# A two-block layer: even blocks of the modulation product, first products without the norm, and 32 in place of 28 quarter units ahead of the neighbourhood attention

## What is computed

```python
u = rmsnorm(h, norm_mix_pre)
proj = u @ w_in
q_na, k_na, v_na, q_gl, k_gl, v_gl, g_gl, z_gl = parts
o_na = rmsnorm(neighbourhood_attention(q_na, k_na, v_na, rpb), na_gain)
o_gl = gla_bidirectional(q_gl, k_gl, v_gl, g_gl, z_gl, ...)
h = h + rmsnorm(concatenate([o_na, o_gl]) @ w_o, norm_mix_post)
...
mod = silu(c) @ w_ada + b_ada
```

## Time and profile before

| | |
|---|---|
| median of three runs | 1654.26 us (1652.23 to 1655.45) |
| the profiled execution | 1651.1 us |
| its span, first to last instruction | 1649.3 us |
| mean granted clock of TensorE | 0.959 |
| TensorE busy | 1541.9 us, 93% |
| VectorE, ScalarE, GpSimd busy | 846.0, 630.7, 563.6 us |
| HBM read | 151.89 MB, 93 GB/s over the span |

### The profile page before, as it was taken

The page is one execution under the profiler, slowest core; times in us unless marked ns, Lnnn a source line. Parts: engine busy times, 40 slices in busy tenths (PEclk is TensorE's granted clock), DMA queues, the critical chain, the costliest instruction groups (busy, mean ns, idle before and its releaser), DMA issues.

```text
span 1649.3 us, 20836 instructions
## 1 busy us (share of the span) xinstructions
PE 1541.9 (93%) x8734; PEld 1303.8 (79%) x8734; DVE 846.0 (51%) x1081; ACT 630.7 (38%) x1008; POOL 563.6 (34%) x231
## 2 busy tenths in 40 slices
PE   4979899987999999998999998999988999999996
PEld 4978788886999999876768766777876888888885
DVE  3243232425788888744569757863454343342122
ACT  4452534644333333322342345345444333233231
POOL 2321121131444444533324422222442444444441
PEclk9999899797999999999799998999998999999998
DMA  4211111011222232766222211111221333332332
GB/s 178 90 52 40 39 63 67 22 65 39 91 90 91 95 96 92 258 243 241 86 77 90 94 60 51 65 52 51 90 77 63 129 115 128 111 99 97 103 102 77
DMA packets 43628, 155.32 MB, mean 94 GB/s; under 512 B 4848, under 2 KB 5488, under 8 KB 43536
## 3 DMA queue, kind: packets, MB, share of 16 engines
q1 hardware_dynamic: 42960, 151.51, 26.8%
q10 hardware_dynamic: 576, 2.49, 0.4%
HBM read 151.89 MB, written 2.10 MB: 93 GB/s over the span
## 4 chain that ended last, share of the span: by engine, by line
PE 84%; ACT 6%; DVE 5%; DMA 2%; issue 1%; POOL 0%; SPq 0%; DVEq 0%; ACTq 0%
PE G L410 72%; DMA raw<-wstream 2%; PE B L387 2%; PE B L857 1%; PE B L877 1%; DVE ada_acc L1712 1%; PE B L769 1%; PE G L643 1%; PE B L602 1%; ACT whi L954 1%; PE G L550 1%; PE G L867 1%; PE G L645 1%; PE B L515 1%; PE B L619 0%
## 5 line engine op out<-in xcount | busy, mean ns | idle before, releaser
L367 POOL TENSOR_TENSOR wlo<-raw,whi 128x1024 fp32r<-128x1024 f32 x227 | 563.4, 2485 | 1058.0 <-ACT whi L954 1058.0
L410 PE MATMUL G<-uhi,whi 128*128 128x258 f32 (+4 forms) x1920 | 539.0, 333 | 36.9 <-DVE ulo L1437 12.3
L410 PE MATMUL G<-ulo,whi 128*128 128x258 f32 (+4 forms) x1920 | 527.0, 327 | 0.0
L410 PE MATMUL G<-uhi,wlo 128*128 128x258 f32 (+4 forms) x1920 | 525.9, 326 | 0.0
L410 PEld LDWEIGHTS G<-uhi,whi 128*128 128x128 f32 x1920 | 325.4, 192 | 104.1 <-issue 67.4
L410 PEld LDWEIGHTS G<-uhi,wlo 128*128 128x128 f32 x1920 | 325.6, 192 | 30.1
L410 PEld LDWEIGHTS G<-ulo,whi 128*128 128x128 f32 x1920 | 325.5, 192 | 28.1
L954 ACT ACTIVATE whi<-raw 128x1024 fp32r<-128x1024 f32 x227 | 239.4, 1055 | 222.7 <-DMA raw<-wstream 222.5
L410 PE MATMUL G<-yhi,whi 128*128 128x512 f32 x352 | 142.0, 404 | 12.5 <-POOL wlo L367 12.5
L410 PE MATMUL G<-ylo,whi 128*128 128x512 f32 x352 | 141.4, 402 | 0.0
L410 PE MATMUL G<-yhi,wlo 128*128 128x512 f32 x352 | 140.9, 400 | 0.0
(11 more groups left out here) (266 smaller groups left out, 1588.8 us busy)
## 6 DMA issues: line engine op xcount, KB each, us to landing
raw<-wstream SPq DMA_DIRECT2D x227, 512.0 KB, 3.3
ada_in<-ada SPq DMA_DIRECT2D x40, 512.0 KB, 5.9
ada_late<-ada SPq DMA_DIRECT2D x8, 512.0 KB, 3.6
h<-hT SPq DMA_DIRECT2D x8, 264.0 KB, 4.5
out<-res SPq DMA_DIRECT2D x8, 256.0 KB, 2.1
biasn<-bias SPq DMA_DIRECT2D x2, 960.0 KB, 10.8
...
```

Of the source, the lines that this page charges most:

```text
L367: pool.tensor_tensor(wlo[:, i, :], raw[:, i, :], whi[:, i, :].bitcast(F32), ALU.subtract)\
L410: ins = pe.matmul(dst[:, x, 0:xw], w[:, slot, b * P:(b + 1) * P], u[:, k, off + x0:off + x0 + xw], start=(first and i == 0 and j == 0), st ...
```

## The change

The first products use `h * gain` without the root; the copy out of PSUM multiplies each token by its root instead. Lists and buffers: g comes first among the mixed units, 32 pieces run ahead of the neighbourhood attention, squares have three buffers, `tx` has four and lies where q comes later. SP's order at the start and the steps of the modulation blocks change, and DVE splits the first two units in place of POOL.

```diff
-MIXED = [("q", 0), ("k", 0), ("v", 0), ("g", 0), ("g", 1), ("g", 2), ("g", 3),
+MIXED = [("g", 0), ("g", 1), ("g", 2), ("g", 3), ("q", 0), ("k", 0), ("v", 0),
          ("q", 1), ("k", 1), ("v", 1), ("q", 2), ("k", 2), ("v", 2), ("q", 3), ("k", 3), ("v", 3)]
-GLA_PIECES = 28
-NA_SHARE = [3, 2, 3, 2, 3, 3, 2, 3, 2, 3, 3, 3, 2, 2, 0, 0, 0, 0]
+GLA_PIECES = 32
+NA_SHARE = [2, 2, 2, 2, 2, 3, 3, 2, 2, 3, 3, 3, 2, 1, 0, 0, 0, 0]
...
+def ada_by(j):
+
+    return min(ADA_EARLY, ADA_RING + 5 * j // 3)
...
+        sg = sb("sg", [P, 4, T], arena(o))
+        zT = sb("zT", [32, T], arena(o))
+        sq1 = sb("sq1", [P, 3, T], arena(o + 2112)); o += 8448
...
+        tx = sb("tx", [P, 4, T], arena(0)); o += 4224
...
+        rstd1 = sb("rstd1", [P, T], arena(o)); o += 2112
...
+        ADDED = ("mix_pre", "mix_post", "ffn_post", "ffn2", "final")
...
-            for k in range(KD):
-                sp.dma_start(h[:, k, :], hT[:, k, :]).then_inc(s[f"h_in{k % 2}"], 16)
-            sp.dma_start(vec[:, :], vecs).then_inc(s["vec_in"], 16)
-            sp.dma_start(ones[:, :], consts[:, P:2 * P]).then_inc(s["ones_in"], 16)
+            sp.dma_start(vec[:, 0:KD], vecs[:, 0:KD]).then_inc(s["pre_in"], 16)
+
+            def load_h(k):
+                sp.dma_start(h[:, k, :], hT[:, k, :]).then_inc(s[f"h_in{k}"], 16)
...
-            for n in range(RING):
-                load_unit(n)
+            load_unit(0)
+            load_h(0)
+            load_unit(1)
+            load_h(1)
+            load_h(2)
+            for k in range(3, KD):
+                sp.wait_ge(s[f"h_in{k - 3}"], 16)
+                load_h(k)
+            sp.dma_start(vec[:, KD:NVEC], vecs[:, KD:NVEC]).then_inc(s["vec_in"], 16)
+            sp.dma_start(ones[:, :], consts[:, P:2 * P]).then_inc(s["ones_in"], 16)
+            sp.wait_ge(s["h_in5"], 16)
+            load_unit(2)
+            sp.dma_start(upt[:, :], up).then_inc(s["up_in"], 16)
+            sp.dma_start(scan_keep[:, :, :], scanm).then_inc(s["gla_in"], 16)
+            load_unit(3)
+            sp.wait_ge(s["unit_in2"], 16)
             sp.dma_start(ident[:, :], consts[:, 0:P]).then_inc(s["ident_in"], 16)
-            sp.dma_start(scan_keep[:, :, :], scanm).then_inc(s["gla_in"], 16)
...
-                    for x in range(ADA_RING + 2 * j - 2, min(ADA_EARLY, ADA_RING + 2 * j)):
+                    for x in range(ada_by(j - 1), ada_by(j)):
...
-            for n in range(NUNIT):
+            pool.wait_ge(s["unit_split"], 2)
+            for n in range(2, NUNIT):
```

```diff
+            two_tiles(U0["z"], T0["z"], lambda k: split_ready("mix_pre", k))
+
+            def half_tile(dst, n, half):
+
+                unit_ready(n)
+                ins = product(dst, n % RING, [(k, k) for k in range(4 * half, 4 * half + 4)], uhi, ulo, 0, T,
+                              first=(half == 0), last=(half == 1))
+                if half == 1:
+                    ins.then_inc(s["unit_used"], 1)
+
+            q_last = U0["q_gl"] + 1
+            half_tile(B4[:, 2:4], q_last, 0)
...
             sums("mix_pre")
-            two_tiles(U0["z"], T0["z"], lambda k: split_ready("mix_pre", k))
-            for name in ("q_gl", "k_gl"):
-                for i in range(1 if name == "q_gl" else 0, 2):
-                    fm_tile(U0[name] + i, T0[name] + i)
...
+            half_tile(B4[:, 2:4], q_last, 1)
+
             def gate_logits(j):
-                if j >= 2:
+                if j == 0:
+                    pe.wait_ge(s["up_in"], 16)
+                    pe.wait_ge(s["ln_done"], 1)
...
             gate_logits(0)
+            pe.wait_ge(s["evac_done"], T0["z"] + 1)
+            half_tile(G[:, 0], U0["k_gl"], 0)
             gate_logits(1)
+            half_tile(G[:, 0], U0["k_gl"], 1)
+            gate_logits(2)
+            pe.wait_ge(s["evac_done"], T0["q_gl"] + 1)
+            half_tile(G[:, 1], U0["k_gl"] + 1, 0)
+            gate_logits(3)
+            half_tile(G[:, 1], U0["k_gl"] + 1, 1)
...
-                fm_tile(U0["v_gl"] + i, T0["v_gl"] + i)
-                if i < 2:
-                    gate_logits(i + 2)
+                unit_ready(U0["v_gl"] + i)
+                pe.wait_ge(s["evac_done"], T0["k_gl"] + 1 + i)
+                product(G[:, i % 2], (U0["v_gl"] + i) % RING, [(k, k) for k in range(KD)], uhi, ulo, 0, T)\
+                    .then_inc(s["unit_used"], 1)
...
-            piece(27)
+            for x in range(27, 30):
+                piece(x)
             pe.wait_ge(s["amat_done"], 5)
             for hh in range(GLA_H):
+                if hh >= 2:
+                    piece(28 + hh)
```

```diff
-            def h_here(k):
-                act.wait_ge(s[f"h_in{k % 2}"], 16 * (k // 2) + 16)
+            ln_and_exp()
+            act.wait_ge(s["pre_in"], 16)
+            hi_through(0)
+            for k in range(KD):
+                act.wait_ge(s[f"h_in{k}"], 16)
+                act.activation(uhi[:, k, :], h[:, k, :], ACT.Copy, scale=v("mix_pre", k)).then_inc(s["uhi_done"], 1)
+                if k == 0:
+                    hi_through(1)
+                square("mix_pre", k, h[:, k, :])
+            hi_through(3)
             act.wait_ge(s["vec_in"], 16)
-            act.activation(csilu, v("c", 0, 8), ACT.Silu).then_inc(s["csilu"], 1)
-            squares("mix_pre", lambda k: h[:, k, :], h_here)
-            hi_through(2)
             root("mix_pre")
...
+            def gate_log(j):
 
                 b = j % 2
+                if j >= 2:
+                    act.wait_ge(s["gate_low"], j - 1)
                 act.wait_ge(s["gate_x"], j + 1)
...
+            def gate_exp(j):
+
                 act.wait_ge(s["gate_b"], 2 * j + 1)
...
+                act.activation(qdec[:, j, :], kend[:, j, :], ACT.Exp, scale=1.0 / 16).then_inc(s["gate_eb"], 1)
+                act.activation(kinv[:, j, :], kend[:, j, :], ACT.Exp, scale=-1.0 / 16).then_inc(s["gate_eb"], 1)
...
                 act.wait_ge(s["gate_b"], 2 * j + 2)
-                act.activation(tx[:, b, :], tx[:, b, :], ACT.Exp, scale=1.0 / 16).then_inc(s["gate_ed"], 1)
...
+                act.activation(tx[:, j, :], tx[:, j, :], ACT.Exp, scale=1.0 / 16).then_inc(s["gate_ed"], 1)
+
+            hi_through(5)
+            gate_log(0)
+            hi_through(6)
+            gate_log(1)
+            gate_exp(0)
+            hi_through(7)
+            gate_log(2)
+            gate_exp(1)
+            hi_through(8)
+            gate_log(3)
+            gate_exp(2)
+            hi_through(9)
+            gate_exp(3)
+            hi_through(12)
...
+                if x % 4 == 3:
+                    i = x // 4
+                    hi_through(U0["mixed"] + i + RING - 1)
+                    if i == 4:
+                        act.wait_ge(s["evac_done"], T0["mixed"] + 4)
+                        act.activation(csilu, v("c", 0, 8), ACT.Silu).then_inc(s["csilu"], 1)
+                        act.activation(sg[:, :, :], sg[:, :, :], ACT.Silu).then_inc(s["sg_done"], 1)
+                        ln_and_exp()
...
-            after_piece(27)
+            for x in range(27, 32):
+                after_piece(x)
...
-                hi_through(U0["ffn_out"] + 3 * c + RING + 1)
+                hi_through(U0["ffn_out"] + 3 * c + RING)
                 act.wait_ge(s["unit_used"], U0["ffn_out"] + 3 * c + 3)
                 act.activation(m2[:, c, :], G[:, t % 2, 0, :], ACT.Copy).then_inc(s["evac_done"], 1)
+                hi_through(U0["ffn_out"] + 3 * c + RING + 1)
```

```diff
+            def split_unit(n):
+                dve.wait_ge(s["unit_hi"], n + 1)
+                dve.tensor_tensor(wlo[:, n, :], raw[:, n, :], whi[:, n, :].bitcast(F32), ALU.subtract)\
+                   .then_inc(s["unit_split"], 1)
+
+            def first_low(k):
+                dve.wait_ge(s["uhi_done"], k + 1)
+                dve.scalar_tensor_tensor(ulo[:, k, :], h[:, k, :], v("mix_pre", k), uhi[:, k, :].bitcast(F32),
+                                         ALU.mult, ALU.subtract).then_inc(s["ulo_done"], 1)
+
+            dve.wait_ge(s["pre_in"], 16)
+            split_unit(0)
+            first_low(0)
+            split_unit(1)
+            for k in range(1, KD):
+                first_low(k)
+                add_square("mix_pre", k)
+
+            def normed(dst, bank, rows=P):
+
+                dve.tensor_tensor(dst.rearrange("p (x w) -> p x w", x=2), bank[0:rows, :, 0:T // 2],
+                                  rstd1[0:rows, :].rearrange("p (x w) -> p x w", x=2), ALU.mult).then_inc(s["evac_done"], 1)
+
+            def normed_qkv(name, i, dst, bank):
+                dve.wait_ge(s["unit_used"], U0[name] + i + 1)
+                normed(dst[:, i, :], bank)
+
...
+            def gate_scan(j):
...
+            def gate_out(j):
+
+                hp = j % 2
                 dve.wait_ge(s["gate_eb"], 2 * j + 2)
-                dve.tensor_tensor(kinv[:, j, :], kgl[:, hp, :], te[:, b, :], ALU.mult).then_inc(s["gate_used"], 1)
```

(50 more changed lines are left out.)

118 lines of the change are left out of this document (44 added, 74 removed).

## The result

The changed kernel takes **1596.8 us** (median of four runs, 1595.82 to 1600.78) against 1653.32 before (four runs, 1652.23 to 1655.45): ratio 0.9661, 95% interval 0.9641 to 0.9681. The forecast was 1601. The profiled execution took 1596.32, its span is 1594.5 (before 1649.3), and the granted clock is 0.968 in place of 0.959. So 54.8 us of span went; the forecast had 53.2.

The account below looks back on a forecast made before the run. TensorE has work 93% of the span, so time is won only where it stands still or runs at the lower clock. Gains sum to 53.2 us: 1651.1 to 1597.9, plus 3.2 for the median, 1601; own range 1595 to 1607.

Parts of the forecast that it names:

- start, to the logits: Start: no norm ahead of the products and a new load order bring the logits from 50.4 to 30.2, gain 20.2 us.
- gates, to the first mixed piece: Gates: ACT's waits for the v_gl copies leave the gates as DVE takes the copies, gain 10 us.
- mixed units: Mixed units: copies move from ACT to DVE and g comes first, gain 0.5 us, bounds -2 and +1.
- ahead of the neighbourhood attention: Passage from gated to neighbourhood attention: table loads go, pieces 28 to 31 come in, gain 3.5 us, bounds 0 and 6.
- neighbourhood attention: Neighbourhood attention: 32 pieces in place of 36, relief counted earlier, DVE 37% busy; zero gain, bounds -4 and +2.
- ffn_out: ffn_out: five blocks per tile in place of six end PE's waits for `wlo`; gain 19 us, bounds 0 and 19.7.
- the term for the cold clock: Start: about 3 us of first products at the lower clock, counted as 1.4 us in the eight steps.
- Rival (c): Start: late or cold, gain 14 us in place of 20, kernel 1607; chance 0.07.
- rival (b): Gates: DVE bounds them if POOL meets all two-input products, 8 to 12 us lost, kernel 1611; chance 0.13.
- together 14.8: Ahead of the neighbourhood attention: pieces, sums of squares, Ln and Exp, from last gated value to root's end, 14.8 us.
- rival (d): Neighbourhood attention: copies and softmax share DVE's queue, engines work one after another, 75 us more, kernel 1676; chance 0.02.
- Rival (a): ffn_out: modulation blocks come late and hold DVE's squares' sum and ACT; half the gain lost, kernel 1611; chance 0.13.

Follow-up runs that it names:

- experiment 5: The changed kernel with the old order of loads at the start, all eight h tiles ahead of units 0 and 1: 1603.36 us, ratio 0.9708.
- experiment 9: The changed kernel with the first two units' splits put back on POOL in place of DVE: 1599.66 us, ratio 0.9654.
- Experiment 6: The changed kernel with 28 extra matmuls on zeros ahead of the first product: 1605.47 us, ratio 0.971.
- Experiment 7: The changed kernel with the four sums of squares moved ahead, behind piece 27, piece 28 before the fourth: 1598.0 us, ratio 0.9665.
- experiment 4: The changed kernel with 28 pieces ahead of the neighbourhood attention in place of 32, and the old shares: 1589.81 us, ratio 0.962.
- Experiment 8: The changed kernel with one piece moved from step 6 to step 13 of the neighbourhood attention: 1591.18 us, ratio 0.9628.
- experiment 1: The changed kernel with the old schedule of the modulation blocks, ACT's new order in ffn_out kept: 1623.83 us, ratio 0.981.
- experiment 3: The kernel before with the even schedule of the modulation blocks and nothing else: 1635.92 us, ratio 0.9894.
- experiment 2: The changed kernel with ACT's old order in ffn_out, unit 3c + 5 rounded ahead of the copy of tile c: 1595.79 us, ratio 0.9635.

## Why the prediction was right, and where its terms were off

Every time below is of the two profiled executions.

| term | forecast | measured |
|---|---|---|
| start, to the logits (50.4 to 30.26) | 20.2 | 20.1 |
| gates, to the first mixed piece | 10 | 9.3 |
| mixed units | 0.5 | 1.1 |
| ahead of the neighbourhood attention | 3.5 | 1.6 |
| neighbourhood attention | 0 | 4.6 |
| gated feed-forward up to ffn_out | not named | 0.8 |
| ffn_out | 19 | 19.7 |
| behind ffn_out | not named | -2.5 |
| sum | 53.2 | 54.7 |

The mechanisms came as forecast in the start, the gates and ffn_out, which make 49 of the 55 us. That the sum fits within 2 us is in part luck: what I had at nothing or not at all, 5.4 and -2.5, nearly cancels the 1.9 lost ahead of the neighbourhood attention, and the clock alone moves the attention by up to 10 us from one execution to the next (last section).

**Start.** The first product was forecast at 10.1 and came at 9.93. DVE's splits took 1.23 (I had 1.28), and from the first product to the logits it took 20.3 us (forecast 20.1). My estimate of unit 1's landing, 7.3 to 7.5, fits after (7.52), but the same start has it up to 8.83 in other executions, and the first product at up to 11.25: that 9.93 came so near is luck of this one. Experiments 5 and 9 show what the two helpers give: the order of the loads 5 to 7 us, DVE's split up to 2.0 behind the unit. Experiment 6 measures the term for the cold clock: 1.6, forecast 1.4. Rival (c) is out.

**Gates.** 41.25 us for 40.5. DVE did not become the bound: rival (b) priced every two-input product as hit, but in the trace of after they were hit one at a time, as each unit of POOL (2.4 to 2.7 us) meets one instruction. The timeline of DVE shows which:

```profile
43.65 2.36 DVE L1570 TENSOR_TENSOR tx<-kend 128x16 f32<-128x16 f32 x1
...
51.77 2.79 DVE L1568 TENSOR_TENSOR tx<-kend 128x512 f32<-128x512 f32 x1
...
57.77 3.34 DVE L1563 TENSOR_TENSOR_SCAN kend<-scan_keep,tx 128x528 f32<-128x528 f32 x1
...
64.31 2.73 DVE L1577 SCALAR_TENSOR_TENSOR qdec<-qgl,qdec 128x528 f32<-128x528 f32 x1
```

POOL started units at 43.24, 51.61, 57.53 and 64.09. Their neighbours of the same shape stayed at 0.69 to 0.70, the scan at 1.26, the copy of 16 columns at 0.16 to 0.17. The copies out of PSUM were never hit, as I had taken from the earlier trace rows: this one, still running when POOL's 2.38 us began at 150.95, took what the other eleven take (q, k and v: 1.065 to 1.100):

```profile
150.57 1.07 DVE L1611 TENSOR_TENSOR vT<-G,rstd 128x512 f32<-128x512 f32 x1
```

By the rule in the Trainium skill (SBUF — State Buffer, Who interferes with whom), that two SBUF inputs contend and one does not, both were to be expected, and the traces of this case agree. What I had mis-sized was the copy of a mixed tile, with its strided order: 1.09 plus 0.08 for the meta columns, against my 0.7 to 0.9.

**Ahead of the neighbourhood attention.** The mis-sized term: "together 14.8" for what runs from the last gated value to the end of the root was 16.8 (147.36 to 164.19). Of the 2.0 us, 1.35 are PE's pause for the copy of tile v, which my sum did not have, and the rest are the sums of squares, four at 0.9 in place of 0.75. PE stands 4.50 there where I had about 5. Experiment 7 shows that the chain can't simply be reordered; experiment 4 that the four pieces weren't worth the place: with 28 the pause is shorter. What I argued, that a piece moved out of a busy stage is a gain in full if its place is idle, holds only for an idle place, and these four pieces stand in front of a chain that PE then waits for. That this is why they gained so little is argued; what is measured is the 1 us of experiment 4.

**Neighbourhood attention.** Zero was forecast, 4.6 came, beyond the three pieces. DVE did 16.58 us in 40 in place of 11.96, 41% where I had 37%, and PE was as busy as before: rival (d) is out. The gain, counted up to the product of w_o that waits for the attention's last low parts (at 339.37 before and 302.61 after), is smaller pauses, 6.6 in place of 10.3 us from step 1 on, and the rest clock. Most of these 3.7 us, 2.4, closed behind the attention, where PE waited 2.03 and 3.10 us in w_o and now waits 2.71. But this term hides one of the other sign, which no row of before could show me: thinner steps at the end, and the clock after them. Experiment 8 takes 5.6 us out of the whole kernel with one piece.

**ffn_out.** The stage is ffn_out2's, 122.86 against 122.95. Experiments 1 and 3 show the cause from both sides: with the even steps in before the pauses go, without them in after they return. Rival (a), a late block, didn't occur. My step "ACT copies tile c before it waits for unit 3c + 5" named a help that wasn't needed (experiment 2).

**Behind ffn_out.** I had costed this at nothing, without a row for it. The stage's last matmul to the first product of the next took 27.8 us, and now takes 30.04. The timeline of after:

```profile
748.16 1.05 ACT L999 ACTIVATE whi<-raw 128x1024 fp32r<-128x1024 f32 x1
...
749.11 0.62 ACT L1021 ACTIVATE sq<-m 128x512 f32<-128x512 f32 x1
749.28 2.35 POOL L387 TENSOR_TENSOR wlo<-raw,whi 128x1024 fp32r<-128x1024 f32 x1 [2.20 <-ACT whi L999]
749.76 2.42 DVE L1494 TENSOR_TENSOR rstd<-rstd,sq 128x512 f32<-128x512 f32 x1 [4.93 <-ACT sq L1021]
```

ACT's new order puts a unit's rounding ahead of the last square, and its end starts POOL just in time to meet DVE's addition of that square (2.42 for 0.7). Experiment 2, without it, gets 0.7 of the 2.2 back. The other 1.5 go with the clock: 17.1 us at the lower one where before has 13.7, and half of the difference is 1.7. The longer stretch goes with no single part of the change: experiment 3, with ACT's old order and the blocks alone, has 17.1 us and 29.44, and experiment 1, with the old blocks, 17.1 and 30.16. Why before's one trace has less stays open.

**Clock.** In all, the records show TensorE at 1.2 GHz for 102.7 us in the execution after and 133.6 before. With the 4 us or so of after's first products, for which there is no record, half of the difference, about 14 of the 55 us, is clock. The forecast took it in as part of the start (1.4 us), the gates (1.3) and ffn_out, and had no term for it elsewhere.
